# A two-block float32 network on one core: modulation k-tiles one at a time and earlier, and a quarter of the low parts on GpSimd

## The reference, cut to what matters

```python
h = rms_norm(x, norm_g) @ w_in          # even and odd layer: the wide projections
...
sc, scc = jax.nn.silu(c), jax.nn.silu(c_ctx)
shift, scale, gate = jnp.split(sc @ mod_w[i] + mod_b[i], 3, axis=-1)
cshift, cscale, cgate = jnp.split(scc @ mod_w[i] + mod_b[i], 3, axis=-1)
```

## Time and profile before

| | |
|---|---|
| median of three runs | 2607.85 us (2606.51 to 2608.6) |
| the profiled execution's own time | 2616.21 us |
| its span (first to last instruction) | 2613.9 us |
| TensorE busy | 2499.0 us, 96% |
| VectorE busy | 1555.0 us, 59% |
| ScalarE busy | 1170.8 us, 45% |
| GpSimd busy | 230.7 us, 9% |
| mean DMA rate | 163 GB/s, 425.22 MB |

### The profile page before, as it was taken

One profiled execution on the slowest core, in us unless ns is written; L12 is line 12 of the kernel. 1 busy time (PEld: TensorE's weight loads), 2 busy tenths in 40 slices (PEclk: granted clock), 3 DMA queues, 4 the chain that ended last, 5 costly groups with the idle time before them and its releaser, 6 DMA issues.

```text
span 2613.9 us, 31326 instructions
## 1 busy us (share of the span) xinstructions
PE 2499.0 (96%) x11888; PEld 1975.3 (76%) x11888; DVE 1555.0 (59%) x2092; ACT 1170.8 (45%) x1719; POOL 230.7 (9%) x126
## 2 busy tenths in 40 slices
PE   6999999999998999999999999899799999999988
PEld 5887777777776777788777777787687877878767
DVE  4644456656776676566767767633546374654754
ACT  6454344643543334356565555422425344252542
POOL 0000000000000000012645544000000000000000
PEclk9999999999999999999999999999899999999989
DMA  5558777637677887764333332223234233342323
GB/s 216 182 181 277 238 251 256 228 107 251 228 265 243 288 275 274 265 223 140 105 92 93 96 92 92 97 95 98 82 97 129 89 121 97 96 130 88 121 81 129
DMA packets 275122, 425.22 MB, mean 163 GB/s; under 512 B 14374, under 2 KB 92988, under 8 KB 273852
## 3 DMA queue, kind: packets, MB, share of 16 engines
q1 hardware_dynamic: 273596, 418.09, 48.6%
q10 hardware_dynamic: 1408, 5.51, 0.6%
HBM read 421.45 MB, written 2.10 MB: 162 GB/s over the span
## 4 chain that ended last, share of the span: by engine, by line
PE 84%; DVE 5%; ACT 4%; DMA 4%; issue 2%; SPq 1%; ACTq 0%; DVEq 0%
PE ps L751 58%; PE ps L1143 12%; DMA ring<-in_od_w_in 3%; PE ps L1126 2%; PE ps L824 2%; ACT ring_hi L1362 2%; DVE ring_lo L1816 1%; PE ps L913 1%; PE ps L802 1%; PE ps L1237 1%; DVE mem_kv L1932 1%; PE ps L1255 1%; PE ps L940 1%; PE ps L1098 1%; PE ps L843 1%
## 5 line engine op out<-in xcount | busy, mean ns | idle before, releaser
L1362 ACT CAST ring_hi<-ring 128x1024 fp32r<-128x1024 f32 (+2 forms) x590 | 611.5, 1039 | 1094.4 <-PE ps L751 608.3
L1816 DVE TENSOR_TENSOR ring_lo<-ring,ring_hi 128x1024 fp32r<-128x1024 f32 (+2 forms) x526 | 635.0, 1214 | 748.1 <-ACT ring_hi L1362 744.5
L751 PE MATMUL ps<-ring_hi,act_hi 128*128 128x512 f32 (+2 forms) x1272 | 515.1, 405 | 23.5 <-DVE ring_lo L1816 12.8
L751 PE MATMUL ps<-ring_hi,act_lo 128*128 128x512 f32 (+2 forms) x1272 | 496.2, 390 | 0.0
L751 PE MATMUL ps<-ring_lo,act_hi 128*128 128x512 f32 (+2 forms) x1272 | 495.9, 390 | 0.0
L751 PE MATMUL ps<-ring_hi,features_hi 128*128 128x512 f32 x1152 | 463.1, 402 | 17.0 <-DVE features_lo L2278 7.4
L751 PE MATMUL ps<-ring_lo,features_hi 128*128 128x512 f32 x1152 | 453.5, 394 | 0.0
L751 PE MATMUL ps<-ring_hi,features_lo 128*128 128x512 f32 x1152 | 453.5, 394 | 0.0
L751 PEld LDWEIGHTS ps<-ring_hi,act_hi 128*128 128x128 f32 x1272 | 242.6, 191 | 110.5 <-issue 34.5
L751 PEld LDWEIGHTS ps<-ring_hi,features_hi 128*128 128x128 f32 x1152 | 219.1, 190 | 88.5 <-issue 32.2
L751 PEld LDWEIGHTS ps<-ring_hi,act_lo 128*128 128x128 f32 x1272 | 242.9, 191 | 51.2
(11 more groups left out here) (251 smaller groups left out, 2497.7 us busy)
## 6 DMA issues: line engine op xcount, KB each, us to landing
ring<-in_mod_w SPq DMA_DIRECT2D x192, 512.0 KB, 5.2
ring<-in_att_w_in SPq DMA_DIRECT2D x128, 512.0 KB, 3.5
ring<-in_ev_w_in SPq DMA_DIRECT2D x104, 512.0 KB, 4.8
ring<-in_od_w_in SPq DMA_DIRECT2D x96, 512.0 KB, 5.5
ring<-in_lru_w_in SPq DMA_DIRECT2D x64, 512.0 KB, 4.0
ring<-in_ev_w_out SPq DMA_DIRECT2D x40, 512.0 KB, 3.9
ring<-in_od_w_out SPq DMA_DIRECT2D x36, 512.0 KB, 4.7
ring<-in_lru_w_out SPq DMA_DIRECT2D x32, 512.0 KB, 3.4
```

The costliest lines, as they stand in the source:

```text
L751: mm = pe.matmul(PS[:, bank, 0:n], a, w[:, k - k0, :], start=(k == k_first and j == 0), stop=(k == k_last and j == 2))
L1362: act.copy(high(U, n), raw(U, n)).then_inc(s_hi, 1)
L1816: dve.tensor_tensor(out=low(U, n), in0=raw(U, n), in1=high(U, n).bitcast(F32), op=ALU.subtract).then_inc(s_lo, 1)
```

## The change

Three things, all in tables and in the order of instructions; no arithmetic is added or taken away.

1. `VTILES_BY` says for each split unit which VectorE k-tiles are done at it. Before, both k-tiles of a vmod unit were done when `follow` came to that unit. Now the four k-tiles of a pair are done one each at four successive split units, beginning four split units before the pair (`_at` is the number of split units before the pair, less 4), and never before an earlier k-tile.
2. `POOL_LO`: of the split units from the 89th `ev_b` unit of the table (U = 56) to the last before `od_out` (U = 489) every fourth low part is made by GpSimd. These are 60 units: 22 of `ev_b`, 1 `uq`, 1 `ukv`, 10 `ev_out`, 24 `od_b`, 2 `od_c`. VectorE's `lo_to` leaves them out.
3. On GpSimd the four copies that double the odd layer's keys (line 2547 before) stand between two of these low parts.

```diff
+POOL_LO = []
...
-    _pool = _name == "lru_in"
+    _pool = _name == "lru_in" or POS["ev_b", 88] <= POS[_name, _u] < UNIT0["od_out"] and sum(_made) % 4 == 3
+    if _pool and _name != "lru_in":
+        POOL_LO.append(POS[_name, _u])
...
-SUMMED_BESIDE = {min((s, m) for s, m in SUMS_BY.items() if s > POS["vmod", 8 * p + 7])[1]: p for p in range(N_VMOD)}
+VTILES_BY = {}
+_last = 0
+for _u in range(0, 8 * N_VMOD, 2):
+    _at = sum(s < POS["vmod", _u] for s in SPLIT_UNITS) - 4
+    for _j in range(4):
+        _last = max(_last, _at + _j)
+        VTILES_BY.setdefault(SPLIT_UNITS[_last], []).append((_u + _j // 2, _j % 2))
+    assert _last < _at + 5
+VTILE_LAST = {unit: U for U, tiles in VTILES_BY.items() for unit, _ in tiles}
+SUMMED_BESIDE = {min((s, m) for s, m in SUMS_BY.items() if s > VTILE_LAST[8 * p + 7])[1]: p for p in range(N_VMOD)}
...
                     U = SPLIT_UNITS[s]
-                    lo(U, unit_width(*RING[U]))
+                    if not LO_BY[U][0]:
+                        lo(U, unit_width(*RING[U]))
...
-            def mod_products(unit):
-                p, j = divmod(unit[1], 8)
-                U, n = POS[unit], wanted(N_MOD + p)
-                done = VMOD_STEPS[unit] - 2 * n
+            def mod_product(u, half):
+                p, j = divmod(u, 8)
+                U, n, k = POS["vmod", u], wanted(N_MOD + p), 2 * j + half
+                done = VMOD_STEPS["vmod", u] - (2 - half) * n
...
                 dve.wait_ge(s_w[U % SLOTS], landed(U))
...
-                    if unit in VMOD_STEPS:
-                        mod_products(unit)
+                    for tile in VTILES_BY.get(U, ()):
+                        mod_product(*tile)
...
+            keys_at = min(U for U in POOL_LO if U > POS["od_b", 8 * 8 + 4])
+            for U in POOL_LO:
+                if U == keys_at:
+                    pool.wait_ge(s_rope, roped("swa0"))
...
+                weights_lo(U, n=unit_width(*RING[U]))
```

More of the change, by code:

```diff
@@ L1914, in mod_columns @@
                 ins.then_inc(s_modd, 1)
-            def mod_products(unit):
-                p, j = divmod(unit[1], 8)
-                U, n = POS[unit], wanted(N_MOD + p)
-                done = VMOD_STEPS[unit] - 2 * n
-                if j == 0 and p >= 2:
+            def mod_product(u, half):
+                p, j = divmod(u, 8)
+                U, n, k = POS["vmod", u], wanted(N_MOD + p), 2 * j + half
+                done = VMOD_STEPS["vmod", u] - (2 - half) * n
+                if k == 0 and p >= 2:
                     dve.wait_ge(s_modt, {q: m for m, q in SUMMED_BESIDE.items()}[p - 2] + 1)
                 dve.wait_ge(s_w[U % SLOTS], landed(U))
[L1924 to L1934, removed]
+                rows = raw(U)[:, half * CHUNK:(half + 1) * CHUNK]
+                for w in range(n):
+                    acc, by = VACC[:, p % 2, w if n == 2 else half, :], CS[:, 2 * k + w:2 * k + w + 1]
+                    if j == 0 and (k == 0 or n == 1):
+                        ins = dve.tensor_scalar(acc, rows, by, None, ALU.mult)
+                    else:
+                        dve.wait_ge(s_vmod, done - 1)
+                        ins = dve.scalar_tensor_tensor(out=acc, in0=rows, scalar=by, in1=acc, op0=ALU.mult, op1=ALU.add)
+                    ins.then_inc(s_vmod, 1)
+                    done += 1
             def ropes_behind(stage, u):
@@ L2537, in _, with weights_lo @@
         def _(pool):
-            def weights_lo(U, i=None):
+            def weights_lo(U, i=None, n=UNIT):
                 pool.wait_ge(s_hi, at(SPLIT_BEFORE[U] + 1, i, 8))
-                pool.tensor_tensor(out=low(U), in0=raw(U), in1=high(U).bitcast(F32),
+                pool.tensor_tensor(out=low(U, n), in0=raw(U, n), in1=high(U, n).bitcast(F32),
                                    op=ALU.subtract).then_inc(s_lop, 1)
[L2544 to L2548, removed]
+            keys_at = min(U for U in POOL_LO if U > POS["od_b", 8 * 8 + 4])
+            for U in POOL_LO:
+                if U == keys_at:
+                    pool.wait_ge(s_rope, roped("swa0"))
+                    for j in range(2):
+                        for z in range(2):
+                            ins = pool.tensor_copy(KD[:, j, :, 64 * z:64 * z + 64], HO[:, :, OD_KC + 64 * j:OD_KC + 64 * j + SWA_DH])
+                    ins.then_inc(s_kd, 1)
+                weights_lo(U, n=unit_width(*RING[U]))
             def block_vectors(b, n):
```

## The result

The changed kernel is slower: 2621.88 us, the median of 20 runs (2614.18 to 2630.99), against 2610.03 (2603.67 to 2616.75, 20 runs) for the kernel before beside it; ratio 1.0048, 95% interval 1.0036 to 1.006. The forecast was 2596.4 us, and the range ended at 2611. The profiled execution of the changed kernel, 2615.18 us, is one of its quickest, and that of the kernel before, 2616.21 us, one of its slowest. So the two profiles end nearly together, and what they show is where time is waited for, not the whole 12 us.

A forecast was written before the change was run, and what follows sets the result against it. TensorE, busy 96%, was taken as the bound, its idle time coming from helpers waiting for the ring and the ring for VectorE. -15.6 + 3.0 + 3.9 + 0 - 2.7 = -11.4 us, from the median 2607.85 to 2596.4; range 2581 to 2611.

The forecast's parts named there:

- A new wait: K-tiles taken early wait for their unit to land, low parts and TensorE behind them: +3.0 us, 0 to 7.
- Low parts on GpSimd: 60 low parts take about 2.47 us instead of 1.21, about 3 of them late for TensorE: +3.9 us, 0 to 43.
- What it does to VectorE: GpSimd low parts spare VectorE work but block it, -1.2 to +1.3 us each: 0 on the path, +5 at most.
- VectorE's busy time: Sign: VectorE's busy time stays within 30 us of 1555.
- rival 1: GpSimd blocks VectorE, which becomes the bound from 700 to 850 us, share above 75%: +9, 2617 us; chance 0.15.
- The k-tiles, earlier and single: Ring slots come free earlier and VectorE's product blocks go, shortening TensorE's waits: -15.6 us, bounds 0 and 24.6.
- Clock: Fewer gaps remove a quarter of TensorE's low-clock loss: -2.7 us of 10.8; clock 0.98 or better from 700 to 1110 us.
- The queue's wait for VectorE: Sign: the issuing queue's wait for VectorE's products falls from 84.7 us to below 20.
- at 26 us or grows: Sign that the forecast is wrong: TensorE's idle time from 600 to 1110 us stays at 26 us or grows.
- TensorE's wait for sums: Sign: TensorE's wait for the modulation sums, 5.0 us before, goes to under 2 us.

The follow-up runs named there:

- the cap: Changed kernel, but no k-tile taken while its unit lies behind the next low part's: 2596.17 us, 0.994; with all low parts on VectorE 2591.92 us, 0.9928.
- GpSimd alone: The kernel before with the same 60 low parts on GpSimd, k-tiles where they were: 2623.04 us, ratio 1.0037.
- the k-tiles alone: The changed kernel with every low part on VectorE again and GpSimd's copies as before: 2619.06 us, ratio 1.0024.
- Sums first: The changed kernel with the bias rows' copy and the sums ahead of the k-tiles of the same unit: 2606.47 us, ratio 0.998.

## Why the prediction was wrong

The step that failed is **"A new wait"**, 3.0 us with an upper end of 7; without the cap it cost 25. Two things were wrong in it. I counted only the low part behind the waiting k-tile, and found for the rest that "VectorE would have waited for the ring anyhow". But behind it also stand the sums, the bias rows' copy and the heads' steps, whose inputs have nothing to do with the ring's head, and for which TensorE has already run dry. And I judged the distance from one place, unit 383, which comes just behind 382, the unit of the next low part, and counted four such places. By the table 38 of the 128 k-tiles belong to a unit behind that of the next low part, 34 by one unit and four by two or four (the three that stalled by 2, 1 and 4); six of them are taken 8 or 10 units ahead, so that with 8 slots the k-tile's slot still belongs to the unit at which it is taken, or to a later one. And where TensorE lags, six ahead is too far as well (unit 350). Measured: 1.0024 less 0.9928, 25 us. The two traces show 18.8 us of it as idle time of TensorE from 600 to 1110 us (30.7 against 11.9), 16.2 in the three stalls (5.3, 6.7 and 4.2), and 5.4 us as clock (14.1 against 8.7).

**"Low parts on GpSimd"** (3.9) and **"What it does to VectorE"** (0, at most 5): together 9.7 us on the order of before (0.0037), 6.3 us on the changed order (1.0048 less 1.0024, in two groups), about 3 us on the capped one, not clear of noise. The size is in the range that I gave, the shares aren't shown apart. VectorE's busy time fell by 18.7 us where 60 x 1.21 = 73 us of work left, so each GpSimd low part gave (73 - 18.7) / 60 = 0.9 us back as blocking: +0.9 less 1.21 is -0.3 us, in my interval of -1.2 to +1.3, below the half in which I looked for it. It fell mostly on the products (747 to 915 ns, 34 us) and not, as I wrote, on the low parts (1.21 to 1.245 us, not 1.5; 15 us). An example of lateness and blocking together is unit 385, the one that I named. The changed kernel there, GpSimd, VectorE, TensorE:

```profile
906.83 2.34 POOL L2552 TENSOR_TENSOR ring_lo<-ring,ring_hi 128x1024 fp32r<-128x1024 f32 x1 [14.76 <-ACT ring_hi L1373]
...
908.07 2.19 DVE L1827 TENSOR_TENSOR ring_lo<-ring,ring_hi 128x1024 fp32r<-128x1024 f32 x1 [2.09 <-ACT ring_hi L1373]
...
909.23 0.50 PE L762 MATMUL ps<-ring_hi,act_hi 128*128 128x512 f32 x1 [2.33 <-POOL ring_lo L2552]
```

TensorE waited 2.33 us instead of 0.35. About half of this is lateness (2.34 instead of 1.21 us for the low part). The rest is that TensorE was there 3.4 us earlier than before (906.90 against 910.30) and the unit's high part only 2.6 us (its cast began at 905.70 against 908.28). VectorE's low part beside it took 2.19 us and ended 1.09 us after GpSimd's, nearly the 1.22 us of an undisturbed one. It is so without exception where it can be seen: in the trace of "GpSimd alone" 14 of VectorE's low parts that the timeline from 200 to 1110 us shows one by one began while one of GpSimd's ran. All ended 1.07 to 1.09 us after it, whether they had begun 0.14 or 2.36 us before its end. The rule of the Trainium skill (SBUF — State Buffer, "Who interferes with whom") that the two engines exclude each other is borne out. My rival 1 built on it asked for a full VectorE, and that did not come: 66% from 700 to 850 us, not above 75. The sign was rival 1's. Its mechanism, blocking, is there, but what GpSimd costs in all is at most 6 to 10 us, and without GpSimd the three stalls are the same.

**"The k-tiles, earlier and single"** (-15.6) and **"Clock"** (-2.7) were right in kind, for another kernel. The queue's wait for VectorE fell to 13.9 us as said. Where nothing waits ahead of the ring, the two came to -0.0072, 19 us, against 18.3 predicted; that they agree so well is partly luck, as the shares were wrong both ways: TensorE's waits for sums hardly fell (5.0 to 4.5 us, where I had taken all of them), and those for head copies fell by 5.3 us (3.8 to 1.4 and 3.6 to 0.7), where I had taken 2.5. I had also read one row wrongly: VectorE's idle time of 3.98 us lies behind the low part of 382, so only one of the four products moved into it, not the two that go ahead of 382. In the changed kernel the clock term had the other sign: 0.95, 0.97 and 0.92 instead of 0.98. Of the signs that I named, idle time "at 26 us or grows" came (29.8), and with it the clock; the queue's wait for VectorE and VectorE's busy time (1536.3 us) came out as forecast, and TensorE's wait for sums rose to 8.1 us instead of falling below 2.

The steps add up along one path: the k-tiles under the cap -19 us, taking the cap away +25, GpSimd +6, in all +12, as measured. This is by differences of the same kernels, so it accounts for the time and proves nothing by itself. What shows the cause is that one condition turns the sign and takes the three stalls away, and that the same reordering of the sums is worth 18 us or nothing by whether the products wait.

Left open: what part of GpSimd's price is blocking and what is lateness; and whether a start of five or six split units without blocks, or a cap by slots instead of by low parts, gives more. None of these was tried.

## What to carry to other kernels

When work is moved earlier on an in-order engine, ask two things of every place, not of one: is its input's buffer still held by a slower consumer, and which instructions stand behind it whose inputs are ready. Put a bound in units of the ring, not in units of the engine's own work, and keep blocks short enough to fit into the consumer's lead. Here an engine with 30% idle time had little use for a helper that blocked it: of 73 us taken off VectorE 51 to 54 came back.

## What the runs showed of the hardware

A stall of TensorE cost more than its length. In the changed kernel, after the 5.39 us of idle time before 840.46, matmuls begin 0.43 us apart, before it 0.23:

```profile
834.45 0.39 PE L762 MATMUL ps<-ring_lo,act_hi 128*128 128x512 f32 x1
834.68 0.39 PE L762 MATMUL ps<-ring_hi,act_lo 128*128 128x512 f32 x1
...
841.05 0.63 PE L762 MATMUL ps<-ring_lo,act_hi 128*128 128x512 f32 x1
841.47 0.63 PE L762 MATMUL ps<-ring_hi,act_lo 128*128 128x512 f32 x1
```

That is the lower of the two levels, 1.2 instead of 2.4 GHz; the granted clock is 0.53 from 840.5 to 846 us, and from 845.7 us on matmuls are 0.23 us apart again. All three long stalls of this trace are followed by such a stretch, of 3.5 to 5.3 us. But not every such stretch follows a stall: there are six more from 600 to 1110 us, and seven in the trace of before, of 2.5 to 3.2 us.

So one trace says little of what stalls cost in clock. By the count used above, the k-tiles alone lose 14.1 us with the same three stalls with which the changed kernel loses 22.8, and "Sums first" loses 24.0 with fewer. The mean granted clock of all runs of a kernel is steadier: 0.983 for the kernel before in each group, 0.980 for both kernels with the three stalls (20 and 12 runs), 0.983 for "Sums first" (10), 0.984 to 0.985 for the capped order, with all low parts on VectorE or 60 on GpSimd (6 runs each time). The step from 0.983 to 0.980 is worth about 8 us of 2600, an estimate.

A GpSimd subtraction of 128 x 1024 that nobody read raised VectorE's mean low part from 1214 to 1240 ns and its mean product from 746 to 787 ns, 26 of them among 702 instructions: 526 x 0.026 + 176 x 0.041 = 21 us. With VectorE's other instructions it was 25.0 us, 0.96 us for each.
